# Expert layers: 64 tokens by gathered rows on VectorE, 192 in the dense products with the tokens as moving side

## What is computed

```python
def peer_ffn(x, wq, keys, u, v):      # cut: per chunk of 128 tokens
    q = (xc @ wq).reshape(c, PEER_HEADS, 2, half)               # 8 heads
    sc = jnp.einsum('thid,ikd->thik', q, keys)                  # 2 x 128 keys
    top_s, top_i = lax.top_k(sc, PEER_TOPK)                     # 16 of each half
    cand_s = top_s[:, :, 0, :, None] + top_s[:, :, 1, None, :]
    cand_i = top_i[:, :, 0, :, None] * PEER_NKEYS + top_i[:, :, 1, None, :]
    best_s, best_pos = lax.top_k(cand_s.reshape(c, PEER_HEADS, -1), PEER_TOPK)
    idx = jnp.take_along_axis(cand_i.reshape(c, PEER_HEADS, -1), best_pos, axis=-1)
    gate = jax.nn.softmax(best_s, axis=-1)
    ue, ve = u[idx], v[idx]            # u, v: 16384 x 1024 each
    act = jax.nn.gelu(jnp.einsum('td,thkd->thk', xc, ue), approximate=False)
    return jnp.einsum('thk,thkd->td', gate * act, ve)
```

## Time and profile before

| | |
|---|---|
| median of 3 executions | 3053.89 us (3053.79 to 3056.28) |
| span of the profiled execution | 3056.4 us, first to last instruction; with this profile no time outside the span is given, so the span stands for its own time |
| PE busy | 2975.8 us, 97% |
| DVE, ACT, POOL busy | 76%, 49%, 10% |
| moved from HBM | 438 MB, 144 GB/s over the span |
| granted TensorE clock, mean | 0.991 of 2.4 GHz |

### The profile page before, as it was taken

How to read it: one execution, slowest core, us unless ns; L and a number is a source line. 1 busy time by engine, 2 the same in 40 slices (tenths; PEclk the granted TensorE clock), 3 DMA queues, 4 the chain that set the end, 5 groups by cost and what they waited for, 6 DMA issues and landing times.

```text
span 3056.4 us, 51698 instructions
## 1 busy us (share of the span) xinstructions
PE 2975.8 (97%) x16532; PEld 2524.8 (83%) x16532; DVE 2327.6 (76%) x5236; ACT 1488.7 (49%) x2689; POOL 295.2 (10%) x413
## 2 busy tenths in 40 slices
PE   8999999999989999999999999999999999999999
PEld 5888887879887879888888888778798888888887
DVE  6888888466656867997777777778679977777776
ACT  4222323245745655275555554456552755555544
POOL 0000000000000005191000000000051910000000
PEclk9999999999999999999999999999999999999999
DMA  7233332223222334313554555523344145555553
GB/s 284 112 120 124 111 127 106 83 87 138 83 97 97 125 124 166 138 56 140 190 190 182 190 188 210 179 99 123 138 152 138 59 149 191 182 190 190 182 197 131
DMA packets 75563, 440.84 MB, mean 144 GB/s; under 512 B 7024, under 2 KB 7408, under 8 KB 35760
## 3 DMA queue, kind: packets, MB, share of 16 engines
q1 hardware_dynamic: 72768, 420.23, 38.2%
q0 software_dynamic: 2672, 19.01, 1.7%
HBM read 438.16 MB, written 1.05 MB: 144 GB/s over the span
## 4 chain that ended last, share of the span: by engine, by line
PE 90%; DVE 4%; issue 2%; ACT 2%; DVEq 1%; DMA 0%; ACTq 0%; POOL 0%; POOLq 0%
PE bank L481 18%; PE bank L483 18%; PE bank L482 17%; PE bank L2488 10%; PE bank L2490 5%; PE bank L2418 5%; PE bank L2450 4%; PE bank L2436 3%; PE bank L1640 2%; PE bank L984 1%; PE bank L973 1%; PE bank L1357 1%; PE bank L1375 1%; DVE arena L1697 1%; PE bank L568 0%
## 5 line engine op out<-in xcount | busy, mean ns | idle before, releaser
L460 ACT ACTIVATE peer_r<-wring 128x512 fp32r<-128x512 f32 x1336 | 830.5, 631 | 801.3 <-PE bank L483 543.2
L465 DVE TENSOR_TENSOR peer_r<-wring,peer_r 128x512 fp32r<-128x512 f32 x1272 | 860.6, 691 | 392.6 <-ACT peer_r L460 388.4
L2488 PE MATMUL bank<-res_r,peer_r 128*128 128x512 f32 x1280 | 457.1, 397 | 3.4 <-DVE peer_r L465 3.4
L481 PE MATMUL bank<-peer_r 128*128 128x512 f32 x1024 | 404.2, 395 | 2.8 <-DVE peer_r L2722 2.8
L481 PE MATMUL bank<-h_r,peer_r 128*128 128x512 f32 (+1 forms) x1088 | 397.6, 365 | 4.4 <-DVE h_r L495 3.3
L483 PE MATMUL bank<-peer_r 128*128 128x512 f32 x1024 | 401.2, 392 | 0.0
L482 PE MATMUL bank<-peer_r 128*128 128x512 f32 x1024 | 399.4, 390 | 0.0
L483 PE MATMUL bank<-h_r,peer_r 128*128 128x512 f32 (+1 forms) x1088 | 384.9, 354 | 0.0
L2490 PE MATMUL bank<-res_r,peer_r 128*128 128x256 f32 x1280 | 359.0, 280 | 0.0
L482 PE MATMUL bank<-h_r,peer_r 128*128 128x512 f32 (+1 forms) x960 | 334.2, 348 | 0.0
L2488 PEld LDWEIGHTS bank<-res_r,peer_r 128*128 128x128 f32 x1280 | 240.5, 188 | 61.4 <-DVE peer_r L465 4.0
(11 more groups left out here) (401 smaller groups left out, 4977.6 us busy)
## 6 DMA issues: line engine op xcount, KB each, us to landing
wring<-in_w_peer SPq DMA_DIRECT2D x256, 1024.0 KB, 4.8
wring<-in_w_proj SPq DMA_DIRECT2D x34, 1024.0 KB, 4.8
wring<-in_w_hy SPq DMA_DIRECT2D x32, 1024.0 KB, 5.0
arena<-in_w_ada POOLq DMA_DIRECT2D x16, 1024.0 KB, 5.0
wring<-in_w_out SPq DMA_DIRECT2D x16, 1024.0 KB, 4.8
wring<-in_w_ada SPq DMA_DIRECT2D x8, 1024.0 KB, 9.8
wring<-in_w_hyout SPq DMA_DIRECT2D x8, 1024.0 KB, 4.8
wring<-in_w_q SPq DMA_DIRECT2D x8, 1024.0 KB, 4.8
```

The costliest lines, as they stand in the source:

```text
L460: act.activation(SPLIT[:, buf, 0, :], raw_quarter(name, i, j, q), ACT.Copy).then_inc(split_hi, 1)
L465: v.tensor_tensor(SPLIT[:, buf, 1, :], raw_quarter(name, i, j, q), SPLIT[:, buf, 0, :].bitcast(F32), ALU.subtract).then_inc(split_lo, 1)
L481: pe.matmul(out_ap, w_hi, x_hi, start=start, stop=False, **kw)
L2488: pe.matmul(two_parts(acc[:, :]), SPLIT[:, buf, 0, w], h_both[:, k, :, :], start=(k == 0), stop=False, skip_group_check=True)
```

## The change

Tokens 0 to 63 (`NG`) leave the dense path. For them the kernel gathers rows: POOL issues 64 indirect transfers per layer (`GATHERS`), each of 128 rows of 8 KB (an expert's `u` and `v` side by side, from a new table `experts{l}`), into a ring of four 1 MB slots. The 128 partitions of one gather are 64 tokens x 2 of their choices. For each, DVE multiplies the `u` row with the token and sums (128x1024), ACT takes the Gelu and the gate of that column, and DVE adds the scaled `v` row to an accumulator (128x1024). 10 of these steps stand in the routing of the second 128 tokens, 4 in the gate table, 32 over the 52 main blocks and 19 over the 76 post blocks.

For tokens 64 to 255 (`TD` = 192) the dense path stays, with these differences. `x . u` is plain float32 everywhere, 192 columns wide. `rows_product` is turned round: `v` (split in three-pass parts) is the *stationary* side in eight 128x128 pieces, and the gated activations of 192 tokens are the moving side: 8 x 3 = 24 matmuls of 192 columns. There are 60 early blocks, 16 MID and 52 main ones. The low part of `v` is made half by DVE and half by POOL. The gate table has 48 groups. Routing is done 128 tokens at a time, and the two sums are turned and joined before the layer norm (`fold_done`).

```diff
-EARLY, MID = 36, 12
-MID_NEAR = 8
-PRE_SPLIT = 8
+EARLY, MID = 60, 16
+MID_NEAR = 10
...
+NG = P // 2
+TD = T - NG
+GRING = 4
+GATHERS = PEER_HEADS * TOPK * NG // P
...
+            for half in range(2):
+                pe.wait_ge(sum_act, SUM0 + 2 * l + half + 1)
+                pe.wait_ge(sum_dve, SUM0 + 2 * l + half + 1)
+                for k in range(4 * half, 4 * half + 4):
+                    c = slice((k % 4) * P, (k % 4 + 1) * P)
+                    pe.matmul(mix_acc(1, half)[:, c], SUMS[:, k, NG:TD], ident, start=True, stop=True)
+                    mm = pe.matmul(mix_acc(0, half)[NG:P, c], SUMS[:, k, 0:NG], ident, start=True, stop=True)
+                mm.then_inc(fold_done, 1)
...
+            pe.wait_ge(h_back, HBACK0 + l + 1)
+            for k in range(KT):
+                for copy in range(2):
+                    mm = pe.matmul(bank[6 + k // 4][copy * NG:(copy + 1) * NG, (k % 4) * P:(k % 4 + 1) * P], h[:, k, 0:NG],
+                                   ident, start=True, stop=True)
...
+                for k in range(KT):
+                    mm = pe.matmul(bank[b][:, 0:TD], w[:, k * P:(k + 1) * P], dense(k), start=(k == 0), stop=(k == KT - 1))
+                mm.then_inc(u_done, 1)
+
+            def rows_product(n, par):
+
+                pe.wait_ge(gp_ready, GP0 + BLOCKS * l + n + 3)
+                for k in range(KT):
+                    half, w = k // 4, slice((k % 4) * P, (k % 4 + 1) * P)
+                    if k % 4 == 0:
+                        pe.wait_ge((v_lo0, v_lo1)[half], BLOCKS * l + n + 1)
+                    buf = 2 * par + half
+                    mm = mm3(pe, expert_sum(k), SPLIT[:, buf, 0, w], SPLIT[:, buf, 1, w], GPR[:, par, 0, :], GPR[:, par, 1, :],
                              False, True, skip_group_check=True)
-                mm.then_inc(unit_used, 1)
...
+                mm.then_inc(v_used, 1)
...
+        def value_lo(e, l, n, half):
+
+            e.wait_ge(v_hi, 2 * (BLOCKS * l + n) + half + 1)
+            buf = 2 * (n % 2) + half
+            return e.tensor_tensor(SPLIT[:, buf, 1, :], value_raw(l, n, half), SPLIT[:, buf, 0, :].bitcast(F32),
+                                   ALU.subtract)
...
+        def gather_step(v, l, g):
+
+            if g < GATHERS:
+                slot = g % GRING
+                v.wait_ge(rows_landed[slot], 16 * ((GATHERS // GRING) * l + g // GRING + 1))
+                u = ROWS_IN[:, slot, 0, :]
+                v.scalar_tensor_tensor(u, u, 1.0, XG, ALU.mult, ALU.mult, accum_out=DOT[:, g:g + 1]).then_inc(dot_done, 1)
+            if g:
+                v.wait_ge(gate_done, GATES0 + GATHERS * l + g)
+                v.drain()
+                v.scalar_tensor_tensor(GACC, ROWS_IN[:, (g - 1) % GRING, 1, :], GW[:, g - 1:g], GACC,
+                                       ALU.mult, ALU.add).then_inc(acc_done, 1)
+
+        def gather_rows(pool, l, g):
+
+            slot = g % GRING
+            if g >= GRING:
+                pool.wait_ge(acc_done, ACC0 + GATHERS * l + g - GRING + 1)
+            pool.indirect_dma_start(ROWS_IN[:, slot, :, :].rearrange("p a c -> p (a c)"), None, A[f"experts{l}"],
+                                    bass.IndirectOffsetOnAxis(ap=GIDX[:, g:g + 1], axis=0)).then_inc(rows_landed[slot], 16)
...
+            for n in range(BLOCKS):
+                name, i, j, _ = value_half(l, n, 1)
+                value_lo(pool, l, n, 1).then_inc(v_lo1, 1)
+                if n < MAIN or (n - MAIN) % 2:
+                    pool.wait_ge(v_lo0, BLOCKS * l + n + 1)
+                    pool.drain().then_inc(chunk_done[slot_of(name, i, j)[0]], 1)
+                if n - 1 in VALUES_AT:
+                    issue(VALUES_AT[n - 1] + GRING)
...
+            for n in range(BLOCKS):
+                gate(n)
+                value_lo(v, l, n, 0).then_inc(v_lo0, 1)
+                if n in VALUES_AT:
+                    gather_step(v, l, VALUES_AT[n])
```

More of the change, by code:

```diff
@@ L1478, in tokens_stats @@
                     v.wait_ge(x_turned, half + 1)
+                elif name[:4] == "post":
+                    v.wait_ge(fold_done, 2 * n + half + 1)
                 else:
@@ L1550, in norm2_scalar @@
         def norm2_scalar(act, l):
-            tokens_scalar(act, 2 * l + 2, peer_acc, C["epsh"])
+            act.wait_ge(v_used, BLOCKS * (l + 1) + 2)
+            for half in range(2):
+                act.activation(SUMS2[:, 2 * half, :], bank[4 + 2 * half][:, 0:2 * TD], ACT.Copy).then_inc(sum_act, 1)
+            tokens_scalar(act, 2 * l + 2, mix_acc, C["epsh"])
             for k2 in (1, 3):
@@ L2494, in peer_tensor @@
[L2494 to L2503 removed]
+            pe.wait_ge(gated_done, GATED0 + l + 1)
@@ new lines, in peer_tensor @@
+            first_product(0, 0)
+            first_product(0, 1)
+            with pe.Fori(0, MAIN // RING - 1) as i:
+                for j in range(RING):
+                    first_product(i, j + 2)
+                    rows_product(RING * i + j, j % 2)
+            last = MAIN // RING - 1
+            for j in range(RING):
+                if j + 2 < RING:
+                    first_product(last, j + 2)
+                rows_product(RING * last + j, j % 2)
+            with pe.Fori(0, KEPT // RING - 1) as i:
+                for j in range(RING):
+                    rows_product(MAIN + RING * i + j, j % 2)
@@ new lines, in peer_tensor, with value_half @@
+            for j in range(RING - 1):
+                rows_product(BLOCKS - RING + j, j % 2)
+            pe.wait_ge(gathered, GATHERED0 + l + 1)
+            for half in range(2):
+                for part in range(2):
+                    pe.matmul(mix_acc(0, half)[0:NG, :], ident[:, part * NG:(part + 1) * NG],
+                              GACC[:, half * 512:(half + 1) * 512], start=(part == 0), stop=(part == 1))
+            rows_product(BLOCKS - 1, 1)
+        def value_half(l, n, half):
+            if n < MAIN:
+                i, j = divmod(n, RING)
+                return f"peer{l}", i, j, D + half * UNIT
+            i, j = divmod((n - MAIN) // 2, RING)
+            return f"post{l}", i, j, ((n - MAIN) % 2) * D + half * UNIT
@@ L2657, in peer_vector @@
-            eq, eq2 = EQ.rearrange("p n (k a) -> p (n k) a", a=TOPK), EQ2.rearrange("p n (k a) -> p (n k) a", a=TOPK)
-            for m in range(2):
+                yield
+                for a, row in enumerate(rows):
+                    v.max_index(places[:, a, 0:8], values[:, a, 0:8], row)
+                    v.match_replace(scratch[a], values[:, a, 0:8], row, -3.0e38)
+                    if a == len(rows) // 2:
+                        yield
+                v.drain()
+                yield
```

558 lines of the change are left out of this document (280 added, 278 removed).

## The result

The changed kernel takes 3167.93 us (median of 4 executions, 3151.55 to 3176.95) against 3054.07 for the kernel before in the same session: ratio 1.0365, 95% interval 1.0335 to 1.0395. It is 3.7% slower where 0.8% faster was forecast, and it lies outside the range. The profiled execution is the fastest of the four (3151.55, span 3149.9); against that span the forecast sum of 3033 is 117 us short.

The account below looks back on a forecast made before the run. PE was taken to bound the kernel, with DVE and POOL deciding in post. Terms of +40.5 - 13 - 46 + 3.5 + 0.7 - 1.3 + 4.1 = -11.5 us a layer gave 3030 us, 0.8% faster; range 2945 to 3100.

Parts of the forecast that it names:

- The floor of a weight load: PE matmuls: a step does not go below about 0.11 us, however few columns move; 2.78 us per rows_product.
- Rival B: PE's rows_product: float32r loads hide, the step is 0.089 us and the product 2.14; whole 2962; chance 0.12.
- turning the 64 tokens: Small term on PE: 32 records x 0.11, +3.5 us a layer.
- x . u and stage 2: Stage 2: 60 blocks x 2.59 = 155.5 us on PE, +40.5 a layer, with DVE's routing hidden.
- Stage 3: Gate table stage: PE needs 84 us, DVE 86 with four gather steps; taken as 88, -13 a layer.
- Transfers at nothing: Main: weights and gathers need 316 GB/s where the chip has moved 394, so they were costed at nothing.
- The step that failed in main: Main: POOL and DVE need 4.5 us a block beside PE's 5.37, so PE's 279 us a layer decide.
- Rival C: Gathers' issue on POOL is slow and keeps DVE out; gain gone from 1.1 us, 3170 at 2.5; chance 0.24.
- C or the transfers hold: Sign to watch for: if PE waits in main, the slow gather issue on POOL or late chunks are the case.
- The step that failed in post: Post: DVE and POOL exclude each other, so blocks cost the sum of both engines, 253 us against PE's 211.
- rival A: Post: no exclusion of DVE and POOL to speak of, so 211 us instead of 253; whole 2946; chance 0.13.
- Before the norm: Before the layer norm: a copy out of the banks 0.6 and 32 records x 0.11, +4.1 us a layer.

Follow-up runs that it names:

- e11: Changed kernel with all low-half splits of v on DVE, no gather steps in stage 3, 51 in main and 4 in post: 2931.6 us.
- e2: Changed kernel with the gathers, DVE's gather steps and ACT's gates left out: 2922.7 us.
- e1: Changed kernel in which POOL hands back a chunk's slot by a count of its own split, without a drain: 3076.8 us.
- e4: Changed kernel with all low halves of v split on DVE, POOL only issuing the gathers: 2978.5 us.
- e3: Changed kernel with only the first four gathers of a layer issued, all DVE steps and drains kept, working on those rows again: 3076.1 us.
- e6: Changed kernel with all splits on DVE and MAIN_STEPS 51 instead of 32, so no gather step stands in post: 2935.7 us.
- e10: The kernel of e1 with an unneeded drain on POOL put ahead of each gather's issue: 3071.9 us.

## Why the prediction was wrong

By its own steps:

- *The floor of a weight load* was right: 0.11 us a step at 192 columns, in plain float32 and in float32r. A `rows_product` is 2.68 us, taken as 2.78; an unhindered main block 5.28, taken as 5.37. Rival B is out. The rule of the Trainium skill that was weighed against it ("TensorE: Matmul & The Clock Gate", LDWEIGHTS) gives 107 ns; the rows have 0.11. The forecast's "however few columns move" holds for loads of 128 columns: turning the 64 tokens (L2438, loads of 64 columns) took 1.9 us for its 32 records, 0.06 each, where 3.5 us stood.
- *x . u and stage 2* were right: stage 2 runs from 1171.3 to 1327.9, 157 us for 155.5, with the routing hidden. *Stage 3* took 93 us for 88: its four steps took the charged 1.23 and 1.28 us on DVE, which was busy for 85.8 us where 86 was charged, but with gaps; without the steps it is 84 to 86 (e11, e2). No run says what the gaps are.
- *Transfers at nothing* was right: PE is gapless in main at 316 GB/s without the drains (e1) and even at 391 (e11).
- **The step that failed in main** is "Beside it POOL and DVE need ... 4.5 us a block, under 5.37 even if they never overlap". It added up busy times and issues, and left out the one instruction on POOL that is not counted as busy: the drain that releases the slot. It was in the diff and in the order of the instructions; the forecast never asked what it waits for. It cost 39 us of main a layer, and 91 us of the whole when it was taken away. Rival C, which had the gathers' issue on POOL as the slow part, named the right engine and the wrong instruction: the issue took 1.06 us, and its formula at 1.06 would cost 19 x 0.53 = 10 us a layer, about the whole gain and no more: it explains a kernel that is no faster, not one that is 114 us slower. That its 3170 for X = 2.5 lies beside the measured 3168 is a coincidence, since X was 1.06, and the sign given for a wait in main ("C or the transfers hold") pointed at two causes that e1 rules out. That "slower" had 0.31 was owed to a mechanism that did not come.
- **The step that failed in post** is "the post's blocks are charged with the sum of both engines: 253". The exclusion is real, as forecast, and rival A is out (e4 against e3: 51 us of rest). But PE is not served by an average. The buffers for `v` and the gate are two blocks deep, a step comes in every third or fourth block, and DVE's 2.45 us plus three collisions arrive at once: PE waits up to 3.5 us (e3), then has its 2.68 in the blocks between, which wins nothing back. And such waits are followed by stretches at 1.2 GHz, which the forecast did not have; they cost 26 us in e3, 23 in the kernel after. Together the rest is 287 without transfers (e3) where the forecast had 265.
- *Before the norm* 10.9 us from the last product (2017.3) to the first of L1482 (2028.2), with 3.9 before the change: +7.0 a layer, forecast +4.1. The copy out of the banks is as charged, and the wait for the statistics, 3.57 us, is the 3.56 of before. What was mis-sized is the turning of the sums, 32 records of 0.195 us where 0.11 was charged, 6.3 us for 3.5; why they are slower, at a granted clock of 1.00, no run says:

```profile
2018.32 0.46 PE L1573 MATMUL bank<-const_t,arena 128*128 128x128 f32 x2 [0.74 <-DVE arena L1592]
...
2028.17 3.40 PE L1482 MATMUL bank<-const_t,arena 128*128 128x128 f32 x16 [3.57 <-DVE arena L1517]
```

The sum again, a layer: main and post +55 on the forecast, stage 3 +5, norm +3, stage 2 +1, turning the 64 tokens -1.6: 62.4, for two layers 125. The part ahead of layer 0's expert stages was 4 us shorter in this execution (1162.3 instead of 1166.5), which leaves 121 for the 117 measured; the 4 between them are not assigned.

Not settled: what decides how long the clock stays low after a wait, and what sets the landing time itself. In main the landing time is 8.0 us in the kernel after, 8.3 in e1, 5.6 in e4 with the same gathers, and 9.3 in e6, where they are denser. It was no bound in any of these but through the drain.

## What to carry to other kernels

A drain on the queue that issues indirect transfers is a wait for their landing; hand a buffer back by a count of the operation that used it, or keep compute off that queue. Sum up a block's load on each engine only if the buffers are deep enough to average it: with two blocks of lead a burst of 2.45 us every third or fourth block, stretched by collisions, reached PE, and then cost half as much again or more in clock. And a second engine that shares its access with the first was no help here: taking POOL's half of the splits back to DVE turned 0.7% slower into 2.6% faster.

## What the runs showed of the hardware

- POOL's drain waits for the outstanding indirect transfer: median 8.07 us behind an issue (landing 7.9), 0.87 ahead of it, 1.18 with no transfer out. A TENSOR_TENSOR behind an issue does not wait (1.28 us, 0.3 us after it).
- The indirect issue of 128 rows of 8 KB holds POOL for 1.06 us (0.93 at least), the plain one 0.53. The Trainium skill ("Perfetto Trace Analysis", DMA Instruction — SWDGE (GPSIMD)) says that such a record ends when the descriptors are written and not when the data has moved; the trace agrees that the record ends long before the landing, 0.95 us of record and 7.8 to the landing.
- After a wait of 3.5 us PE ran at 1.2 GHz for about 3.4 us although it was never idle in them (e3), after one of 2.2 us for about 6.9 us (e10). With waits of up to 1.6 us in e4's post the granted clock of the stretch stayed at 1.00.
- Beside a split of 128x512 on POOL (1.3 us) DVE's two-input operations take longer: 1.42 and 1.32 us instead of 0.35, 2.32 instead of 1.23 (e3).
- A float32r matmul with 128x128 weights starts every 0.11 us at 192 columns, and every 0.21 at half clock. By the columns alone, scaled from the 0.119 us of 256 columns, it would be 0.09 and 0.18, so the load is likely what is paid at either level.
